# A hybrid block and a sparse-attention block on one core: position bias rows made between the blocks and spread in one go

## The reference, cut to what matters

```
h = x + hybrid_mixer(rms_norm(x)) ;  h = h + sq_relu_mlp(rms_norm(h)) ;  x = rms_norm(h, final_norm_g)   # block 1
ada = c @ w_ada + b_ada            -> shift1, scale1, gate1, shift2, scale2, gate2                      # block 2
h = rmsnorm(x) * (1 + scale1) + shift1 ;  proj = h @ w_in
y_fox = forgetting_attention(q, k, v, cumsum(log_sigmoid(f + b_forget)))        # 8 heads of 64
y_dsa = softmax over the top 128 keys of  q.k/8 + rel_bias[t5_bucket(t - s)]    # 8 heads of 64
x = x + gate1 * ((sigmoid(gf) * (y_fox @ w_f) + sigmoid(gd) * (y_dsa @ w_d)) @ w_out)
x = x + gate2 * (relu(rmsnorm(x)*(1+scale2)+shift2 @ w_mlp1)^2 @ w_mlp2) ;  return rmsnorm(x, g_final)
```

## Time and profile before

| what | us |
|---|---|
| median of 3 runs (1353.89 to 1354.32) | 1354.23 |
| span of the profiled execution, first to last instruction | 1351.4 |
| PE busy | 1340.5 (99%) |
| DVE busy | 754.1 (56%) |
| ACT busy | 526.0 (39%) |
| POOL busy | 563.0 (42%) |
| DMA queue q1, share of 16 DMA engines | 39.5% |

### The profile page before, as it was taken

How to read it: one execution, slowest core, us unless ns; L and a number is a source line. 1 busy time by engine, 2 the same in 40 slices (tenths; PEclk the granted TensorE clock), 3 DMA queues, 4 the chain that set the end, 5 groups by cost and what they waited for, 6 DMA issues and landing times.

```text
span 1351.4 us, 18070 instructions
## 1 busy us (share of the span) xinstructions
PE 1340.5 (99%) x6380; PEld 1093.9 (81%) x6380; DVE 754.1 (56%) x1085; ACT 526.0 (39%) x830; POOL 563.0 (42%) x230
## 2 busy tenths in 40 slices
PE   9999999999999999999999999999999999999998
PEld 8888878888888888876877777888878888888886
DVE  3555578475664654878788774444463241432355
ACT  6344234322323324254366655322355133142333
POOL 5334334453553635524222223444434534345351
PEclk9999999999999999999999999999999999999999
DMA  7232245555665655423222323333423423324231
GB/s 230 79 93 83 90 124 167 167 172 174 197 175 163 176 150 163 112 92 96 62 63 79 95 64 94 109 94 109 125 71 102 125 76 111 93 79 123 78 94 63
DMA packets 212807, 155.74 MB, mean 115 GB/s; under 512 B 8932, under 2 KB 193760, under 8 KB 212744
## 3 DMA queue, kind: packets, MB, share of 16 engines
q1 hardware_dynamic: 212280, 154.43, 39.5%
q10 hardware_dynamic: 464, 0.48, 0.1%
HBM read 152.75 MB, written 4.74 MB: 117 GB/s over the span
## 4 chain that ended last, share of the span: by engine, by line
PE 53%; DVE 1%; ACT 1%; issue 0%; POOL 0%; ACTq 0%; DVEq 0%
PE ps L580 28%; PE ps L1126 11%; PE ps L1070 3%; PE ps L1007 2%; PE ps L986 1%; PE ps L973 1%; PE ps L1156 1%; PE ps L959 1%; PE ps L960 1%; PE ps L963 0%; PE ps L946 0%; PE ps L920 0%; PE ps L921 0%; PE ps L924 0%; DVE nt L2267 0%
## 5 line engine op out<-in xcount | busy, mean ns | idle before, releaser
L541 POOL TENSOR_TENSOR w_lo<-raw,w_hi 128x1024 fp32r<-128x1024 f32 x222 | 560.0, 2530 | 758.2 <-ACT w_hi L1212 738.1
L580 PE MATMUL ps<-u_hi,w_hi 128*128 128x512 f32 x944 | 378.3, 401 | 0.7 <-POOL w_lo L541 0.5
L580 PE MATMUL ps<-u_hi,w_lo 128*128 128x512 f32 x944 | 368.4, 390 | 0.0
L580 PE MATMUL ps<-u_lo,w_hi 128*128 128x512 f32 x944 | 367.8, 390 | 0.0
L1212 ACT ACTIVATE w_hi<-raw 128x1024 fp32r<-128x1024 f32 x222 | 231.6, 1053 | 290.7 <-PE ps L580 112.5
L580 PEld LDWEIGHTS ps<-u_hi,w_lo 128*128 128x128 f32 x944 | 177.2, 188 | 37.7
L580 PEld LDWEIGHTS ps<-u_hi,w_hi 128*128 128x128 f32 x944 | 178.2, 189 | 36.1 <-issue 1.6
L580 PEld LDWEIGHTS ps<-u_lo,w_hi 128*128 128x128 f32 x944 | 177.6, 188 | 35.2 <-issue 1.0
L580 PE MATMUL ps<-y_hi,w_hi 128*128 128x512 f32 x320 | 125.2, 391 | 0.1
L580 PE MATMUL ps<-y_hi,w_lo 128*128 128x512 f32 x320 | 124.5, 389 | 0.0
L580 PE MATMUL ps<-y_lo,w_hi 128*128 128x512 f32 x320 | 124.5, 389 | 0.0
(11 more groups left out here) (317 smaller groups left out, 1878.4 us busy)
## 6 DMA issues: line engine op xcount, KB each, us to landing
raw<-w_in SPq DMA_DIRECT2D x69, 512.0 KB, 3.8
raw<-w_mlp SPq DMA_DIRECT2D x64, 512.0 KB, 4.0
adaw<-w_ada SPq DMA_DIRECT2D x32, 768.0 KB, 4.5
raw<-w_up SPq DMA_DIRECT2D x32, 512.0 KB, 6.6
raw<-w_down SPq DMA_DIRECT2D x32, 512.0 KB, 6.0
raw<-w_out SPq DMA_DIRECT2D x16, 512.0 KB, 4.4
bias_rows<-bias_rows SPq DMA_DIRECT2D x4, 635.0 KB
xtok<-x SPq DMA_DIRECT2D x4, 512.0 KB, 7.5
```

The costliest lines, as they stand in the source:

```text
L541: pool.tensor_tensor(w_lo[:, s, :], raw[:, s, :], w_hi[:, s, :], ALU.subtract).then_inc(lo_ready[s], 1)
L580: last = pe.matmul(ps[0:cols, bank, :], w[:, s, c], r[:, k, :], start=(k == ks[0] and w is w_hi and r is r_hi), stop=(k == ks[-1] and w is ...
```

## The change

The two products of the bias rows and ACT's copies go from the first retention stage to the border, the two loads behind them go to the end of block 1's mixer, and the write and all four copies inside DRAM go to block 2's list of loads: the write between the two groups of value loads, the four copies one after the other behind `att_loads(1)`. `tab_load(4)` now waits for them. `fbrow`, `oneh` and `rbias` get their own space. At the border `ada_rows(1)` stands where line 607's two products stood; the bias products stand between the two turns of the roots, in PSUM bank 2 and in columns 256 to 384 of bank TR. Some semaphores are merged (`conv_y3` into `conv_taps`, `bfor_in` into `rope_in`, `mean_sq` into `factor`, `fgate_z` into `fgate_log`), with the counts adapted.

```diff
-            sp.dma_start(oneh[:], tab[0:BUCKETS, TAT["onehot"]:...]).then_inc(sem("bias_in"), 16)
-            sp.dma_start(rbias[:], rel_bias_2).then_inc(sem("bias_in"), 16)
...
             ret_loads(1)
-            brow_copy()
             with sp.Fori(2, NQ) as j:
                 ret_loads(j)
-            brow_spread(0)
...
-            brow_spread(1)
             for i in range(KC // 4):
                 for s in range(4):
                     load(st_out, s, i, (whole, cols(w_out, i * 4 * P + s * P)))
                     if i == 1 and s == 2:
                         sp.wait_ge(sem("mix_done"), 1)
                         ada_load(0, 0, 0, 0)
+                        sp.dma_start(oneh[:], ...).then_inc(sem("bias_in"), 16)
+                        sp.dma_start(rbias[:], rel_bias_2).then_inc(sem("bias_in"), 16)
-            brow_spread(2)
...
-            quarter(0)
-            brow_spread(3)
-            with sp.Fori(1, NF - 1) as q:
+            with sp.Fori(0, NF - 1) as q:
                 quarter(q)
...
             def tab_load(p):
                 if p >= 2:
                     sp.wait_ge(sem("att_logit"), 8 * (p - 1))
+                if p == NQ:
+                    sp.wait_ge(sem("brow_out"), 16 * (NQ + 1))
...
             value_loads(0, W2_FV)
+            brow_copy()
             value_loads(1, W2_DV)
             att_loads(0)
             sp.wait_ge(sem("ada_sum"), 4)
-            sp.wait_ge(sem("brow_out"), 16 * (NQ + 1))
             sp.wait_ge(sem("forget_out"), 16)
...
                 att_loads(g)
                 if g >= 2:
                     tab_load(g)
+                if g == 1:
+                    for j in range(NQ):
+                        brow_spread(j)
...
-            def both_sums():
+            def both_sums(between):
...
-                for _ in range(2):
-                    pe.matmul(ps[:, SB, 0:2 * P], ones[:], small[:, 0:2 * P], start=True, stop=True)
+                between()
...
             def bias_rows_made():
                 pe.wait_ge(sem("bias_in"), 32)
-                pe.matmul(ps[0:HEADS, SB, :], rbias[:], oneh[:, 0:T], start=True, stop=True)
-                pe.matmul(ps[0:HEADS, OU, 0:P], rbias[:], oneh[:, T:NREL], ...).then_inc(sem("brow_done"), 1)
+                pe.wait_ge(bank_free[2], st_idx.turn(2, 0))
+                pe.matmul(ps[0:HEADS, 2, :], rbias[:], oneh[:, 0:T], start=True, stop=True)
+                pe.matmul(ps[0:HEADS, TR, 2 * P:3 * P], rbias[:], oneh[:, T:NREL], ...).then_inc(sem("brow_done"), 1)
+            def vectors_turned():
                 pe.wait_ge(sem("vrow_in"), 16 * (len(VECS) - 1))
-                pe.transpose(ps[:, OU, P:P + NVEC], vrow[:], ...).then_inc(sem("brow_done"), 1)
+                pe.transpose(ps[:, OU, 0:NVEC], vrow[:], ...).then_inc(sem("vec_turned"), 1)
...
-            bias_rows_made()
+            vectors_turned()
             unit(st_ret, 1, 0, u_hi, u_lo)
             unit(st_ret, 2, 0, u_hi, u_lo)
-            pe.wait_ge(sem("brow_read"), 2)
...
-            both_sums()
-            ada_rows(1, 0, closes=False)
+            both_sums(lambda: ada_rows(1, 0, closes=False))
             ada_rows(2, 1, opens=False)
             roots_turned(0)
+            bias_rows_made()
             roots_turned(1)
...
                     if m == 2:
                         ada_row_copy(1)
+                    if m == 4:
+                        act.wait_ge(sem("brow_done"), 1)
+                        act.activation(fbrow[:, 0:T], ps[0:HEADS, 2, :], ACT.Copy, scale=HD ** 0.5) ...
+                    if m == 6:
+                        act.activation(fbrow[:, T:NREL], ps[0:HEADS, TR, 2 * P:3 * P], ACT.Copy, ...) ...
...
-            dve.wait_ge(sem("brow_out"), 16)
             wout(st_out, lambda m: 1.0, "x_mixed", "n2", gained=True)
```

More of the change, by code:

```diff
@@ L267, in build @@
         vrow = sb("vrow", [NVEC, P], where=pre)
-        oneh = sb("oneh", [BUCKETS, NREL], where=pre)
-        rbias = sb("rbias", [BUCKETS, HEADS], where=pre)
         pre.close()
@@ L279, in build @@
         gones, pick = sb("gones", [P, 2], where=one), sb("pick", [P, 64], where=one)
+        fbrow = sb("fbrow", [HEADS, NREL], where=one)
+        oneh = sb("oneh", [BUCKETS, NREL], where=one)
+        rbias = sb("rbias", [BUCKETS, HEADS], where=one)
         one.close()
@@ L397, in _ @@
                               ).then_inc(sem("vrow_in"), 16)
[L398 to L400 removed]
+            sp.dma_start(bfor[:], b_forget_2.rearrange("(h a) -> h a", a=1)).then_inc(sem("rope_in"), 16)
             sp.dma_start(rope[:], tab[:, TAT["cos"]:TAT["cos"] + 2 * T].rearrange("p (a t) -> p a t", a=2)
@@ L426, in _ @@
                         ada_load(0, 0, 0, 0)
-            brow_spread(2)
+                        sp.dma_start(oneh[:], tab[0:BUCKETS, TAT["onehot"]:TAT["onehot"] + NREL]
+                                     ).then_inc(sem("bias_in"), 16)
+                        sp.dma_start(rbias[:], rel_bias_2).then_inc(sem("bias_in"), 16)
             def quarter(q, last=False):
@@ L659, in bias_rows_made @@
                 pe.wait_ge(sem("bias_in"), 32)
-                pe.matmul(ps[0:HEADS, SB, :], rbias[:], oneh[:, 0:T], start=True, stop=True)
-                pe.matmul(ps[0:HEADS, OU, 0:P], rbias[:], oneh[:, T:NREL], start=True, stop=True
+                pe.wait_ge(bank_free[2], st_idx.turn(2, 0))
+                pe.matmul(ps[0:HEADS, 2, :], rbias[:], oneh[:, 0:T], start=True, stop=True)
+                pe.matmul(ps[0:HEADS, TR, 2 * P:3 * P], rbias[:], oneh[:, T:NREL], start=True, stop=True
                           ).then_inc(sem("brow_done"), 1)
+            def vectors_turned():
                 pe.wait_ge(sem("vrow_in"), 16 * (len(VECS) - 1))
-                pe.transpose(ps[:, OU, P:P + NVEC], vrow[:], ident[0:NVEC, 0:NVEC]).then_inc(sem("brow_done"), 1)
+                pe.transpose(ps[:, OU, 0:NVEC], vrow[:], ident[0:NVEC, 0:NVEC]).then_inc(sem("vec_turned"), 1)
             def ret_scores(p):
@@ L1015, in value_slot @@
                                 pe.wait_ge(bank_free[i], st_idx.turn(2, 0) if r == 0 and i == 2 else st_val.turn(i, r))
+                                if r == 0 and i == 2:
+                                    pe.wait_ge(sem("brow_read"), 1)
                             last = block(kk, i)
@@ L1272, in norm @@
                         ada_row_copy(1)
+                    if m == 4:
+                        act.wait_ge(sem("brow_done"), 1)
+                        act.activation(fbrow[:, 0:T], ps[0:HEADS, 2, :], ACT.Copy, scale=HD ** 0.5
+                                       ).then_inc(sem("brow_read"), 1)
+                    if m == 6:
+                        act.activation(fbrow[:, T:NREL], ps[0:HEADS, TR, 2 * P:3 * P], ACT.Copy, scale=HD ** 0.5
+                                       ).then_inc(sem("brow_read"), 1)
             for s in range(1, SLOTS):
@@ L1327, in _ @@
             act.activation(r1[:], ps[:, SA, :], ACT.Copy).then_inc(sem("r1_ready"), 1)
[L1328 to L1331, removed]
-            act.activation(vec[:, KC:NVEC], ps[:, OU, P + KC:P + NVEC], ACT.Copy).then_inc(sem("vec_ready"), 1)
+            act.wait_ge(sem("vec_turned"), 1)
+            act.activation(vec[:, KC:NVEC], ps[:, OU, KC:NVEC], ACT.Copy).then_inc(sem("vec_ready"), 1)
             def keys_turned(p):
@@ L1591, in _ @@
             ahead(st_att, 0, 0)
+            act.wait_ge(sem("brow_out"), 16)
             k_hi(0)
@@ L1932, in conv_in @@
                 dve.wait_ge(bank_free[0], st_conv.turn(0, j) + 1)
-                wait(dve, sem("conv_y3"), j)
+                wait(dve, sem("conv_taps"), 3 * j)
                 dve.tensor_tensor(prod[:, 2:T + 2], ps[:, 1, :], ccs[:], ALU.mult).then_inc(sem("prod_ready"), 1)
@@ L2084, in mlp @@
                 dve.tensor_scalar(factor[:], ps[:, SA, :], 1.0 / D, EPS, ALU.mult, ALU.add
-                                  ).then_inc(sem("mean_sq"), 1)
-                dve.wait_ge(sem("mean_sq"), MLPS.index(name) + 1)
+                                  ).then_inc(sem("factor"), 1)
+                dve.wait_ge(sem("factor"), 2 * MLPS.index(name) + 1)
                 dve.reciprocal(factor[:], factor[:]).then_inc(sem("factor"), 1)
-                dve.wait_ge(sem("factor"), MLPS.index(name) + 1)
+                dve.wait_ge(sem("factor"), 2 * MLPS.index(name) + 2)
                 for i in range(2):
```

31 lines of the change are left out of this document (14 added, 17 removed).

## The result

The changed kernel took 1381.45 us, median of 5 runs (1381.12 to 1385.6); the kernel before, on the same chip, 1353.89 us, median of 5 (1352.79 to 1354.32). The ratio is 1.0213, 95% interval 1.0202 to 1.0224: 2.1% slower. The forecast was 1382.9 us, range 1376 to 1389. In every run on record the time lies 1.7 to 1.9 us above the span of its own execution. So the 2.8 us between span and median, given ahead of the prediction, are these 1.8 us and 1.0 us by which the profiled execution of the kernel before was faster than that median.

A forecast was written before the change was run, and what follows sets the result against it. PE's instruction list was taken to bound the kernel. Span 1351.4 - 1.2 (bias products) + 0 (border) + 0 (write, semaphores) + 28.4 (spreads) + 1.5 (clock) = 1380.1, plus 2.8 to the median: 1382.9 us, range 1376 to 1389.

The forecast's parts named there:

- What bounds the kernel: Whole kernel: PE, busy 1340.5 of 1351.4 us, sets the time; work removed is saved, waits are lost in full.
- The bias products out of retention: First retention stage: without the two bias products the vectors' turn starts at 38.08, saving PE 1.17 us.
- The border at 0: Border: row group exchange and added bias products and copies cost 0, bounds -0.3 and +1.2 us.
- the sign that was written down for the bias products costing time: Border: a longer PE wait at line 621 or 890 would show rival (d), up to +1.5 us, 1354.6.
- The spreads on two engines: Second attention load: four spreads share two DMA engines, 12.75 us each; ACT's cast waits 29.1 us, PE stalls 28.4.
- How the load waits: Pair 2's load, issued at 666.95, waits on two engines behind four spreads and lands at 705.0.
- 38 us behind the issue: Sign in the attention: the `w_in` load behind the spreads lands near 38 us after its issue.
- The chain behind the load: Attention: from cast at 705.0 through exponentials to 707.0, DVE to 709.0, PE's `s_step(0, 6)` at 709.1.
- The clock behind the stall: Behind the attention stall: PE restarts at the 1.2 GHz level, costing 1.5 us, bounds 0 and 3.
- The total: Span 1380.1 us; with 2.8 us from span to median 1382.9 us, 2.1% slower.
- The rival of two colliding spreads: Attention: only two of four spreads collide, ACT 3.6 us late, +2.9 us, 1356.0; chance 0.03.
- the rival without collision: Attention: spreads do not share engines, nothing is late, only 1.17 us saved: 1353.1 us; chance 0.10 together with (d).

The follow-up runs named there:

- 128 rows outermost: Changed kernel, its four spreads written with 128 rows outermost from a small separate tensor, same place: 1352.42 us, ratio 0.9993.
- eight heads: Changed kernel with one spread of all eight heads behind `att_loads(1)` in place of four of two: 1353.25 us, ratio 1.0003.
- idle products back: Kernel with 128 rows outermost, the two idle products back at the border and `ada_rows(1)` behind the sums again: 1353.39 us, ratio 1.0004.
- no bias: Kernel with 128 rows outermost and the idle products restored, without the two bias products (bias not computed): 1353.43 us, ratio 0.9996.
- the exchange alone: Kernel before, with only the row group `ada_rows(1)` in place of the two idle products at the border: 1353.01 us, ratio 1.0000.
- the spreads alone with 128 rows outermost: Kernel before, with only the four spreads moved behind `att_loads(1)`, each with rows outermost: 1353.24 us, ratio 1.0003.
- one more wide product: Kernel with 128 rows outermost and idle products restored, plus one unread 256-column product in the middle of `both_sums`: 1352.33 us, ratio 0.9991.
- one spread each: Changed kernel with its two-engine spreads placed one behind each of `att_loads(0)` to `att_loads(3)`: 1355.42 us, ratio 1.0009.
- the filled wait: Changed kernel with PE kept busy in the wait by 42 unread products of 384 columns ahead of `t_step(0, 2)`: 1381.74 us, ratio 1.0218.

## Why the prediction was right

- **What bounds the kernel.** PE's list sets the time, so a wait is lost in full. Right: a wait of 28.8 us, PE's busy time 0.6 us from the old one, 27.9 us more span.
- **The bias products out of retention.** -1.17 forecast, -1.25 measured, and it arrived whole at the border.
- **The border at 0.** Right in the profiled execution, though not by the wait that was named: line 889 follows the turns without a wait for `u_hi`, and the 0.30 us at line 618, by itself, is the sign that was written down for the bias products costing time. They cost none. The forecast missed, however, that the border has two kinds of execution. The lowest runs without a stall are 1351.1 to 1351.5 us where the bias products have left retention (128 rows outermost, eight heads, idle products back, no bias), and 1352.8 or 1352.9 where they have not (the exchange alone, the spreads alone with 128 rows outermost): 1.3 to 1.8 us, about the forecast gain. Two kernels don't fit as well: with one more wide product 1351.8, and with one spread each, where every run had a fall, 1352.4. Falls of the clock take the gain back in the medians, and cost 4.2 us in the profiled run (1355.3 against 1351.1) and up to 6.5 in single runs (1357.6, mean clock 0.994): a term that the sum didn't have. It may be why one of the five runs took 1385.6 us, with the lowest mean clock of the five, 0.985 against 0.987 to 0.989; no profile shows that run.
- **The spreads on two engines.** Right, and the main term: ACT's wait was worked out at 29.1 us and measured at 29.12. The load was forecast to land at 705.0 in the old trace's clock, less what comes earlier, some 703; the cast began at 703.01. Each spread costs 12.1 to 12.8 us where it is one more.
- **How the load waits.** The landing was expected "near 38 us" behind an issue that itself was left in place. Instead SP was held while it issued the spreads: pair 2's load, due at 666.95 - 2.05 = 664.9, went out 14.1 us late, at 679.00, and landed 24.0 us behind that. The sum is the same 38.1: part of the delay lies ahead of the issue. And the issue of this load itself took SP 12.42 us, so that even its part on the free engines moved only at 692. The mechanism in the prediction, a load that is late by its part on two engines alone, is thus half of it: the queue also held the load as a whole. The sign "38 us behind the issue" was wrong, the instant of the landing and the size of the loss were not.
- **The chain behind the load.** 4.1 us forecast from the cast to `s_step(0, 6)`, 4.74 measured. DVE's two scales took 1.62 us instead of 0.95; why is open. The stall of `s_step` was 29.12 where 28.4 stood in the sum.
- **The clock behind the stall.** +1.5 forecast, 0.86 in the difference of the traces and 0.80 by the filled wait. It was over-sized for this execution; the kernel before with the spreads moved shows 2.04 for a wait of the same length, so the bounds of 0 and 3 were fair.
- **The total.** +28.7 us forecast on the span, +27.93 measured. That it is so close is in part luck: the stall was 0.7 us too small and the clock 0.64 too large, which cancel, and the start's first products gave 0.80 that nobody forecast. The step from span to median, 2.8 us, would have been 1.8 plus the profiled execution's distance from the median, here 0.33.

The rival of two colliding spreads was built as an experiment. ACT was late by 4.25 us where 3.6 was forecast, but the time was 1360.98 us and not 1356.0: PE waited 3.9 us instead of 2.9, the border was 3.80 us longer in its profile by a fall of the clock, and behind the wait the low clock cost 1.04 us (1266.12 - 686.79 = 579.33 from PE's turn behind it to the last long stretch, against 578.29 with the wait filled), a term that the rival had at nothing. Nearest to the rival without collision is the kernel with 128 rows outermost, 1353.1 forecast and 1352.42 measured.

## What to carry to other kernels

Before a transfer is put beside others, read the DMA share in a stretch where it runs alone: 0.13 is two of 16 engines, and everything behind it on these two waits for it, however low the average share. In this kernel such transfers had to stand apart, one per slot with slack, or have a large outermost dimension (four in a row cost 29 us with 2 outermost and nothing with 128; the same bytes as one transfer with 8 outermost cost nothing). In a kernel that PE bounds, follow a late load through the list of the engine that casts it: what stands behind the cast in that list, not the weights themselves, was what PE missed.

## What the runs showed of the hardware

- SP's queue takes the first spread at once (0.70 us) and holds SP at the later ones, up to 12.51 us, and at the load behind them, 12.42. The four issues in the changed kernel (min, median and max in ns, first and last start), against 3.75 us for all four with 128 rows outermost:
```profile
L370 SPq DMA_DIRECT2D bias_rows<-bias_rows x4: 702/9428/12514, 646.7 to 666.4; - x4
```
- In the changed kernel the load behind the last two-engine spread starts on the free engines some 9 us before the spread ends, and its last part on the two engines waits for the end.
- PE's granted clock can fall to 0.50 while PE is busy without a gap, 1.3 to 2.1 us behind a stretch of one-column products; one product of 256 columns among them reduced the runs with a fall from 8 of 12 to 1 of 11. That kernel has the lowest median of all, 1352.33 us, 0.09% under the kernel before, which is no difference that can be told with certainty (interval to 1.0000).
- A wait of 28.8 or 28.9 us costs 0.8 to 2.0 us of low clock behind it, and the 18 products at the kernel's start took 3.59 in one execution and 4.18 in another.
